# First stage of a two-block transformer kernel: another order of its work, Toeplitz copies in halves, output powers on POOL

## The chip, the cores and the metric

The kernel runs on one core of a Trainium2 chip. The metric is the device time of one execution in microseconds (us). All data are float32. TensorE (PE) multiplies and transposes into PSUM, which has eight banks; VectorE (DVE), ScalarE (ACT) and GpSimd (POOL) work beside it; SyncE (SP), POOL and ACT issue DMAs. Every engine takes its own instructions in program order and meets the others only at semaphores.

## The reference, cut to what matters

The whole program is two transformer blocks with two layers each, on 256 tokens of width 1024. The change is inside the first layer's mixer, a diagonal state space model (S5) with 64 groups of 16 channels and 64 complex states per group:

```
shift1, scale1, gate1, ... = split(silu(c) @ ada_w[0] + ada_b[0], 6)      # "ada": 1024 x 6144
h   = rms_norm(x, norm1_g[0]) * (1 + scale1) + shift1
mix = s5_mixer(h, lam, log_dt, b, c, d, w_glu, b_glu)                     # states over 256 tokens
x   = x + gate1 * mix
...                                                                      # FFN, MLA layer, second block
```

The mixer is computed in chunks of 8 tokens. Inside a chunk the outputs are a product with a Toeplitz matrix built from one row of kernel values; between chunks 31 states follow each other, and each chunk's state is multiplied into its outputs with "output powers", C times powers 1 to 8 of the poles.

## The kernel before

One program per engine, each written out by hand; nothing reorders it. Steps wait for each other by semaphores; PSUM banks are handed out in turn by `next_bank`, and the one who reads a bank out signals `emptied`. The first stage reaches from the start to the first FFN, some 154 us of 1232. Names used below:

- **ada panels**: 1 MB pieces of `ada_w`. Panels 0 to 23 are three blocks of eight. POOL issues their loads (`ada_load`, L2892) into six slots (two in `aring`, four in `ring`), the load of panel i after PE has taken panel i - 6. PE takes a panel with `ada_panels` (eight rows in the trace). `take_row` (ACT) and `row_columns` (PE) turn a block's result into columns; block 0 gives `gmod`, with which x is modulated. Panels 24 and up are used by DVE, late in the FFN.
- **input powers**: DVE, `input_powers(b)` for b = 0 to 3, each two halves of three `tensor_tensor` of 128x1024. PE transposes them (`inputs`), ACT copies them out to `wT`, and they also give the kernel row (`kernel_rows`, `kernel_columns`, the latter at L739 and L742), which ACT writes to the last slice of `toep` (`take_kernel_columns`).
- **Toeplitz copies**: SP, L1561, seven DMAs from that slice to the seven others, each shifted by 16 partitions, after both halves of the kernel row are there. Seven memsets on POOL (L2901) clear what they leave free. `own_inputs` (PE, L828) multiplies with the result.
- **modulated x**: U in `hT`, two DVE operations of 128x2048, then `chunk_inputs(b)` on PE for b = 0 to 3, which ACT copies to `BU` in `sq`.
- **scan**: DVE, 30 steps of a `tensor_tensor` (L1581, sq<-stat,arena) and a `tensor_reduce` (L1826). It starts when all four `chunk_inputs` are out and ends with `states_ready`.
- **output powers**: DVE, `output_powers(b)`, six `tensor_tensor` of 128x1024 each. b = 0 ahead of the scan, b = 1 cut into 24 small pieces inside it, b = 2 and 3 behind it. Each half signals `ca_ready`.
- **end of the stage**: PE, `state_outputs(0)` and `(1)` (L851), `gelu_columns`, `state_outputs(2)`, the first gate products `glu_part` (L872), `state_outputs(3)`, the rest of the gate products, then the FFN.
- x in natural layout is loaded once more (`xN`, L1543, 1 MB) and transposed to `xT` (L799).

Of the kernel before, what the change touches and what calls it, by code (L numbers as in the profile page):

```python
# [10 lines left out]
ALU = mybir.AluOpType  # L11
# [3 lines left out]
P = 128  # L15
# [148 lines left out]
def blocks_kernel(nc, a, constants, out):  # L164

    ctx = ExitStack()
    with ctx:
# [126 lines left out]
        kern = carve(3072, 1024).rearrange("p (x n) -> p x n", n=P)  # L294
# [15 lines left out]
        row0 = toep[:, L5 - 1, 0:512]  # L310
# [4 lines left out]
        wT = [carve(o + (2 + i) * 2048, 2048).rearrange("p (j i n) -> p j i n", i=2, n=P) for i in range(2)]  # L315
# [23 lines left out]
        xN = sq[:, :].rearrange("p (b d) -> p b d", d=D)  # L339
# [280 lines left out]
        def _(eng):  # L620
# [45 lines left out]

            eng.wait_ge(done("b_landed"), 16 * 2)
            coefficient_columns(0)
            vector_columns(0, "s")

# [34 lines left out]
            def inputs(b):  # L705

                eng.wait_ge(done("ab_ready"), 2 * (b + 1))
                for i in range(2):
                    for h in range(2):
                        eng.wait_ge(*next_bank(("w", b, i, h), "s"))  # L710
                        ps = bank_of(("w", b, i, h)).rearrange("p (j n) -> p j n", n=P)
                        for j in range(4):
                            last = eng.transpose(ps[:, j, :], aB[b % 2][:, i, 4 * h + j, :], ident)  # L713
                        last.then_inc(*fills(("w", b, i, h)))
# [18 lines left out]
            def kernel_columns(i):  # L733
# [7 lines left out]
                for x in range(4):  # L741
                    last = eng.matmul(ps[:, x * P:(x + 1) * P], kern[:, 4 * i + x, :], ident, start=False, stop=True,  # L742
                                      skip_group_check=True)
                last.then_inc(*fills(("kernT", i)))

            def chunk_inputs(b):
# [4 lines left out]
                eng.wait_ge(done("u_ready"), 1)  # L751
                eng.wait_ge(*next_bank(("bu", b), "s"))
                ps = bank_of(("bu", b)).rearrange("p (j i c) -> p j i c", j=BJ, i=2)
                for j in range(BJ):
                    for i in range(2):
                        for r in range(2):
                            last = mm(ps[r * N5:(r + 1) * N5, j, i, :], wT[b % 2][:, j, i, r * N5:(r + 1) * N5],
# [5 lines left out]
            ada_panels(0, 2)  # L763
            eng.wait_ge(done("group_rows_ready"), 1)
# [5 lines left out]
            ada_panels(2, 2)  # L770
            eng.wait_ge(done("const5_landed"), 16)
            eng.wait_ge(done("xc_squares"), 8)
            eng.wait_ge(*next_bank("xstat", "s"))
            mm(bank_of("xstat")[:, 0:L5], con5("same_chunk"), ss[:, 0, :]).then_inc(*fills("xstat"))
            ada_panels(4, 1)
            inputs(0)
            kernel_rows(0)
            ada_panels(5, 1)
# [57 lines left out]
            for i in range(4):  # L836
                own_inputs(i // 2, i % 2)
# [2098 lines left out]
```

## Time and profile before

| | us |
|---|---|
| median of 3 runs (1226.98 to 1230.12) | 1229.67 |
| the profiled execution | 1233.93 |
| its span | 1231.7 |
| between span and execution time | 2.2 |

The page gives PE as busy for 95% of the span, DVE 39%, ACT 23%, POOL 4%. In a timeline a line is one instruction or a run of like ones: start, duration, engine, line of the program, operation, out<-in, count, and in brackets the idle time of the engine before it and what ended it. The chain of waits follows the work that ended last back to the start. PEclk is the clock that TensorE was granted, as a share of 2.4 GHz.

### The profile page before, as it was taken

The numbers are of one execution on the slowest core, as the hardware profiler recorded it, in microseconds if no ns is written. First come the engines' busy times: TensorE is split into PE (matmuls) and PEld (weight loads), VectorE is DVE, ScalarE is ACT, GpSimd is POOL, SyncE is SP. The second block draws the span as 40 slices with busy tenths as digits, with TensorE's granted clock in tenths as the row PEclk, the third lists the DMA queues.
The fourth block names the chain that finished last, engine by engine and source line by source line (L and its number), as shares of the span: only waits on it lengthen the run. The fifth ranks groups of instructions, "written<-read, shape, count | busy, mean of one in ns | idle before, by whom it ended". The sixth has DMA issues, their size and how long they took to land.

```text
span 1231.7 us, 19272 instructions
## 1 busy us (share of the span) xinstructions
PE 1164.1 (95%) x8403; PEld 960.1 (78%) x8403; DVE 480.4 (39%) x950; ACT 283.2 (23%) x674; POOL 52.5 (4%) x73
## 2 busy tenths in 40 slices
PE   5876999999999999999999999999999999999997
PEld 3535788888887867688888888788899767886666
DVE  6896264441313428623000000427364542405431
ACT  4521330000002445612000000233122322004431
POOL 2310001110000000000000000000022000000000
PEclk9987999999999899999999999999999999999989
DMA  9969669987643234163535341544410004543210
GB/s 301 367 184 354 216 224 378 357 332 268 250 161 110 103 120 139 36 211 110 192 109 198 104 169 35 164 137 138 134 57 4 3 1 137 196 146 103 66 37 35
DMA packets 120770, 196.68 MB, mean 160 GB/s; under 512 B 5772, under 2 KB 104750, under 8 KB 113262
## 3 DMA queue, kind: packets, MB, share of 16 engines
q1 hardware_dynamic: 110554, 132.20, 33.2%
q0 software_dynamic: 8336, 59.77, 12.7%
q10 hardware_dynamic: 1796, 3.47, 0.9%
q8 instruction: 67, 1.10, 0.4%
q14 instruction: 17, 0.14, 0.0%
HBM read 192.54 MB, written 1.05 MB: 157 GB/s over the span
## 4 chain that ended last, share of the span: by engine, by line
PE 86%; DVE 6%; DMA 3%; ACT 3%; issue 1%; POOL 0%; SPq 0%; DVEq 0%; ACTq 0%
PE psum L624 64%; PE psum L955 12%; PE psum L872 2%; PE psum L1391 2%; ACT arena L2371 2%; DMA ring<-in_ada_w 2%; DMA aring<-in_ada_w 1%; DVE arena L1581 1%; DVE stat L1630 1%; PE psum L1182 1%; DVE arena L1587 1%; PE psum L851 1%; PE psum L713 1%; DVE hT L1581 1%; PE psum L1152 1%
## 5 line engine op out<-in xcount | busy, mean ns | idle before, releaser
L624 PE MATMUL psum<-hT,ring 128*128 128x256 f32 x1392 | 313.2, 382 | 2.9 <-ACT hT L2371 1.8
L624 PEld LDWEIGHTS psum<-hT,ring 128*128 128x128 f32 x1392 | 263.3, 191 | 43.4 <-issue 7.3
L2371 ACT ACTIVATE arena<-psum 128x256 f32<-128x256 f32 (+5 forms) x215 | 96.9, 476 | 654.4 <-PE psum L624 596.0
L624 PE MATMUL psum<-hT,arena 128*128 128x256 f32 (+1 forms) x960 | 162.8, 337 | 2.7 <-DVE hT L1581 2.5
L624 PEld LDWEIGHTS psum<-hT,arena 128*128 128x128 f32 (+1 forms) x960 | 141.4, 176 | 22.9 <-issue 4.2
L1581 DVE TENSOR_TENSOR arena<-arena,psum 128x256 f32<-128x256 f32 (+1 forms) x75 | 39.2, 536 | 296.4 <-ACT arena L2371 267.2
L624 PE MATMUL psum<-arena 64*64 64x64 f32 (+6 forms) x1996 | 111.3, 247 | 2.3 <-issue 1.9
L624 PEld LDWEIGHTS psum<-arena 64*64 64x64 f32 (+4 forms) x1996 | 89.4, 140 | 18.6 <-issue 15.6
L624 PE MATMUL psum<-ring,arena 128*128 128x256 f32 (+2 forms) x320 | 85.8, 433 | 0.5 <-ACT arena L2371 0.5
L955 PE MATMUL psum<-arena,ring 128*128 128x256 f32 x384 | 85.1, 380 | 0.0
L1587 DVE SCALAR_TENSOR_TENSOR acc<-aring,c_act,acc 128x2048 f32<-128x2048 f32 x28 | 65.8, 2349 | 43.8 <-DMA aring<-in_ada_w 25.4
L955 PEld LDWEIGHTS psum<-arena,ring 128*128 128x128 f32 x384 | 72.7, 190 | 12.3 <-issue 2.5
L624 PEld LDWEIGHTS psum<-ring,arena 128*128 128x128 f32 x320 | 64.5, 203 | 21.2 <-issue 8.3
L955 PE MATMUL psum<-arena 128*128 128x256 f32 x320 | 70.7, 379 | 0.0
L955 PEld LDWEIGHTS psum<-arena 128*128 128x128 f32 x320 | 60.6, 190 | 8.1
L1581 DVE TENSOR_TENSOR arena<-arena 128x512 f32<-128x512 f32 (+8 forms) x94 | 60.6, 662 | 2.3 <-PE psum L624 0.4
L2917 POOL TENSOR_TENSOR arena<-arena 128x1536 f32<-128x1536 f32 x4 | 13.8, 3440 | 545.4 <-DVE arena L1581 533.9
L624 PE MATMUL psum<-arena,ring 128*128 128x256 f32 x160 | 35.0, 380 | 0.5 <-DVE arena L2069 0.5
L624 PEld LDWEIGHTS psum<-arena,ring 128*128 128x128 f32 x160 | 30.3, 190 | 4.8 <-DVE arena L2069 0.8
L2371 ACT ACT_TABLE_LOAD x25 | 32.1, 1283 | 7.7 <-DVE arena L1584 4.8
L2371 ACT ACTIVATE arena<-arena 128x256 f32<-128x256 f32 (+8 forms) x48 | 26.6, 576 | 22.6 <-DVE arena L2312 13.8
L872 PE MATMUL psum<-hT,ring 128*128 128x256 f32 x128 | 28.4, 381 | 1.3 <-DVE hT L1841 1.3
(232 smaller groups left out, 1120.7 us busy)
## 6 DMA issues: line engine op xcount, KB each, us to landing
aring<-in_ada_w POOLq DMA_DIRECT2D x32, 1024.0 KB, 7.6
ring<-in_ada_w POOLq DMA_DIRECT2D x16, 1024.0 KB, 14.9
ring<-in_a_w_in SPq DMA_DIRECT2D x14, 1024.0 KB, 5.4
arena<-in_ffn_w_gate SPq DMA_DIRECT2D x12, 1024.0 KB, 8.2
arena<-in_ffn_w_up SPq DMA_DIRECT2D x12, 1024.0 KB, 8.3
ring<-in_ffn_w_down SPq DMA_DIRECT2D x12, 1024.0 KB, 5.0
ring<-in_ffn_w_gate SPq DMA_DIRECT2D x10, 1024.0 KB, 9.5
ring<-in_ffn_w_up SPq DMA_DIRECT2D x10, 1024.0 KB, 6.6
```

The costliest lines, as they stand in the source:

```text
L624: return eng.matmul(dst, w, x, start=first, stop=last)
L713: last = eng.transpose(ps[:, j, :], aB[b % 2][:, i, 4 * h + j, :], ident)
L851: last = eng.matmul(y5_at(kh, r, k4, x), st[n5, :, i, j], c[n5, j, :, :], start=False, stop=i == 1, skip_group_check=True)
L872: last = eng.matmul(ps[:, m, :], w[:, k, m * P:(m + 1) * P], hT3[:, k, :], start=m == 0 and k == 0, stop=k == KC - 1, skip_group_check=True)
L955: last = eng.matmul(dn[c // 2][:, c % 2, :], w[:, kk, c * P:(c + 1) * P], hid[:, 2 * j + kk, :], start=(j == 0 and kk == 0 and c % 2 == 0) ...
L1152: last = eng.transpose(ps[0:DQK, h, :], x[:, b, 4 * g + h, :], ident)
L1182: eng.matmul(ps[r, 0:T], v1[:, 0, h * DV:(h + 1) * DV], head_t[:, h % 2, 0:T], start=True, stop=False, skip_group_check=True)
L1391: last = eng.matmul(ps[:, j, :], out0[i][0][:, k, j * P:(j + 1) * P], mixT[0][:, k, :], start=(i > 1 and j == 0 and k == 0), stop=(k == (K ...
L1581: return V.tensor_tensor(dst, x, y, op)
L1587: return V.scalar_tensor_tensor(dst, x, s, y, op0, op1)
L2371: return eng.activation(dst, x, f, **k)
L2917: G.tensor_tensor(lt_m7[l % 2], lt7, mask.unsqueeze(1).to_broadcast([P, NU, CR]), ALU.mult)\
```

## The change

- SP: the load of `xN` is gone. The Toeplitz copies go in two halves of 512 columns, seven DMAs each; the first half waits for the first half of the kernel row only.
- PE: `xT` is made by transposing `xC_in`, the chunked x that is loaded anyway, ahead of panel 2. `inputs` is split in two, the panels are spread between its pieces, `kernel_columns(0)` comes before `inputs(2)`, `own_inputs` comes half by half with panels 20 to 23 behind each half. Five 128x256 matmuls on constants (`keep_warm`) follow the first vector columns.
- DVE: three of the seven memsets are at the start; four on POOL at the start. `group_rep` is made after `input_powers(0)`. x is modulated in halves of 32 groups (`u_ready` 1 and 2) with half of `input_powers(3)` between. All output powers are gone.
- POOL: all output powers, eight halves of three `tensor_tensor` of 128x1024, between the panel loads.
- ACT: the copies follow PE's new order. `wT` has three places, `kern` two.

```diff
-            def inputs(b):
-                eng.wait_ge(done("ab_ready"), 2 * (b + 1))
+            def inputs(b, i):
+                eng.wait_ge(done("ab_ready"), 2 * b + i + 1)
...
-            for i in range(4):
-                own_inputs(i // 2, i % 2)
-            ada_panels(20, 4)
+                eng.wait_ge(done(f"toeplitz{i}_landed"), 16 * (L5 - 1))
+                for r in range(2):
+                    own_inputs(i, r)
+                ada_panels(20 + 2 * i, 2)
...
-                eng.wait_ge(done("ca_ready"), 2 * (b + 1) + (BJ - 2 if b else 0))
+                eng.wait_ge(done("ca_ready"), 2 * (b + 1))
...
-            sp.dma_start(xN, a["x"][0].rearrange("(b p) d -> p b d", p=P)).then_inc(done("x_landed"), 16)
...
             for i in range(2):
                 sp.wait_ge(*emptied_at(("kernT", i)))
-            for t in range(L5 - 1):
-                n = P5 * (t + 1)
-                sp.dma_start(toep[P - n:P, t, :], toep[0:n, L5 - 1, :]).then_inc(done("toeplitz_landed"), 16)
+                for t in range(L5 - 1):
+                    n = P5 * (t + 1)
+                    sp.dma_start(toep[P - n:P, t, 512 * i:512 * i + 512], toep[0:n, L5 - 1, 512 * i:512 * i + 512])\
+                      .then_inc(done(f"toeplitz{i}_landed"), 16)
...
+            modulate(0)
+            input_powers(3, (1,))
+            modulate(1)
...
-            output_powers(0)
             for b in range(NB5):
                 eng.wait_ge(*emptied_at(("bu", b)))
...
-            output_powers(2)
-            output_powers(3)
...
+            def output_powers(b, i, temp, loads=(0, 0, 0)):
+
+                js, k9 = slice(b * BJ, (b + 1) * BJ), slice(1, L5 + 1)
+                dst = (ca_re, ca_im)[i][:, js]
+                temp = temp.rearrange("p (j k q) -> p j k q", k=L5, q=P5)
+                if g.last:
+                    eng.wait_ge(*g.last)
+                for n, (to, pw, co) in enumerate(((dst, powr, ct[:, i]), (temp, powi, ct[:, 1 - i]))):
+                    G.tensor_tensor(to, pw[:, k9, js].rearrange("p k j -> p j k").unsqueeze(3).to_broadcast([P, BJ, L5, P5]),
+                                    co[:, js, :].unsqueeze(2).to_broadcast([P, BJ, L5, P5]), ALU.mult).then_inc(*g.step())
+                    ada_loads(loads[n])
+                eng.wait_ge(*g.last)
+                G.tensor_tensor(dst, dst, temp, (ALU.add, ALU.subtract)[i]).then_inc(*g.signals("ca_ready"))
+                ada_loads(loads[2])
...
+            output_powers(0, 1, ahead, (0, 1, 1))
+            eng.wait_ge(done("xc_scaled"), 8)
+            for h in range(2):
+                for y in range(2):
+                    eng.wait_ge(*filled_at(("xT", h, y)))
+            output_powers(0, 0, ahead, (0, 1, 1))
+            ada_loads(5)
+            eng.wait_ge(done("u_ready"), 2)
+            output_powers(1, 0, behind, (0, 1, 1))
+            output_powers(1, 1, behind, (1, 0, 1))
+            ada_loads(1)
+            eng.wait_ge(*filled_at(("bu", 2)))
+            output_powers(2, 0, behind)
+            eng.wait_ge(*filled_at(("kernT", 1)))
+            output_powers(2, 1, behind)
+            for i in range(2):
+                output_powers(3, i, behind)
```

**POOL, from panel 18's load to the last output power.** In the program before, POOL has only loads here; these are panels 16 to 24 and on (bank 3 filled means that PE has finished a block):

```order
L2892 DMA aring<-in_ada_w 128x2048 [waits early_used] x2
L2892 DMA ring<-in_ada_w 128x2048 [waits early_used]
L2892 DMA ring<-in_ada_w 128x2048 [waits bank3_filled]
L2892 DMA ring<-in_ada_w 128x2048 [waits early_used] x2
L2892 DMA aring<-in_ada_w 128x2048 [waits early_used] x2
```

In the changed program the same stretch is (L2912 and L2916 are the output powers, L2894 the loads; the first row is panel 18, the next load panel 19):

```order
L2894 DMA aring<-in_ada_w 128x2048 [waits early_used]
L2912 TENSOR_TENSOR arena<-arena,acc 128x1024 [waits ca_ready,u_ready]
L2912 TENSOR_TENSOR arena<-stat,acc 128x1024
L2894 DMA aring<-in_ada_w 128x2048 [waits early_used]
L2916 TENSOR_TENSOR arena<-arena 128x1024 [waits gpsimd_step]
L2894 DMA ring<-in_ada_w 128x2048 [waits early_used]
L2912 TENSOR_TENSOR arena<-arena,acc 128x1024 [waits ca_ready]
L2894 DMA ring<-in_ada_w 128x2048 [waits bank3_filled]
L2912 TENSOR_TENSOR arena<-stat,acc 128x1024
L2916 TENSOR_TENSOR arena<-arena 128x1024 [waits gpsimd_step]
L2894 DMA ring<-in_ada_w 128x2048 [waits early_used] x2
L2912 TENSOR_TENSOR arena<-arena,acc 128x1024 [waits ca_ready,bank0_filled]
```

Eleven more `tensor_tensor` stand behind the last of these rows, then panel 24. So loads and output powers now hold each other up: panel 19's load waits for PE to take panel 13, which PE does behind `chunk_inputs(3)`, and everything below it waits too.

**PE, around the Toeplitz products.** Before, one wait for all copies stands ahead of all products (L828), and panels 20 to 23 behind them:

```order
L624 MATMUL psum<-aring,c_act 32x512 [waits ada_panel0_landed]
L624 MATMUL psum<-aring,c_act 32x512 x3
L624 MATMUL psum<-aring,c_act 32x512 [waits ada_panel1_landed]
L624 MATMUL psum<-aring,c_act 32x512 x3
L828 MATMUL psum<-arena,hT 32x128 [waits bank7_emptied,bank6_emptied,bank4_emptied,toeplitz_landed,toeplitz_clear]
```

In the changed program (products at L844) each half has its wait and two panels behind it:

```order
L844 MATMUL psum<-arena,hT 32x128 [waits toeplitz0_landed,bank4_emptied,bank5_emptied,toeplitz_clear]
L844 MATMUL psum<-arena,hT 32x128 x15
L844 MATMUL psum<-arena,hT 32x128 [waits bank5_emptied]
L844 MATMUL psum<-arena,hT 32x128 x15
L625 MATMUL psum<-ring,c_act 32x512 [waits ada_panel2_landed]
L625 MATMUL psum<-ring,c_act 32x512 x3
L625 MATMUL psum<-ring,c_act 32x512 [waits ada_panel3_landed]
L625 MATMUL psum<-ring,c_act 32x512 x3
L844 MATMUL psum<-arena,hT 32x128 [waits bank6_emptied,toeplitz1_landed,bank7_emptied]
```

The copies of the first half no longer wait for the second half of the kernel row, and the products no longer stand in front of panels 20 and 21.

## Rows read from the trace of the kernel before

**Rows 1.** The page: busy time by engine, and PE in 40 slices.
```profile
span 1231.7 us, 19272 instructions
PE 1164.1 (95%) x8403; PEld 960.1 (78%) x8403; DVE 480.4 (39%) x950; ACT 283.2 (23%) x674; POOL 52.5 (4%) x73
...
PE   5876999999999999999999999999999999999997
```

**Rows 2.** Chain of waits, 70 to 160 us: start, us, what.
```profile
78.19 14.03 DMA aring<-in_ada_w
...
94.19 7.17 issue
101.36 5.99 PE psum L828 x128
```

**Rows 3.** Windows: stretch, length, then each engine's busy us, clock, DMA share, GB/s.
```profile
84.00:101.00 17.00, 3.87 (x16) 0.40 (x16) 16.24 (x47) 0.00 (x0) 1.06 (x2) 0.55 1.02 310
```

**Rows 4.** Timeline of SP, and the copies' times to landing (L1561).
```profile
75.72 5.56 SPq L1561 DMA_DIRECT2D arena<-arena  x7
...
DMA to landing us min/median/max: 2.9/10.8/20.7
```

**Rows 5.** Timeline of PE, 60 to 150 us.
```profile
68.66 2.06 PE L624 MATMUL psum<-hT,arena 128*64 128x32 f32 x64
70.65 1.12 PE L739 MATMUL psum<-acc,const_sb 16*128 16x512 f32 x2
71.70 1.16 PE L742 MATMUL psum<-const_sb,arena 128*128 128x128 f32 x8
...
112.08 3.36 PE L851 MATMUL psum<-arena 64*32 64x128 f32 x128
...
127.31 1.98 PE L851 MATMUL psum<-arena 64*32 64x128 f32 x64
```

**Rows 6.** Timeline of DVE: first wait, ada columns, output powers, scan steps, output powers again.
```profile
5.74 0.26 DVE L1643 COPY stat<-psum 128x96 f32<-128x96 f32 x1 [4.29 <-PE psum L624]
...
46.31 0.29 DVE L1581 TENSOR_TENSOR arena<-psum,arena 128x128 f32<-128x128 f32 x1 [4.10 <-PE psum L693]
...
71.73 0.29 DVE L1581 TENSOR_TENSOR sq<-stat,arena 128x128 f32<-128x128 f32 x1
...
94.39 0.29 DVE L1581 TENSOR_TENSOR sq<-stat,arena 128x128 f32<-128x128 f32 x1
...
95.12 0.29 DVE L1581 TENSOR_TENSOR sq<-stat,arena 128x128 f32<-128x128 f32 x1
...
98.67 1.21 DVE L1581 TENSOR_TENSOR arena<-arena,acc 128x1024 f32<-128x1024 f32 x1
...
111.64 1.22 DVE L1732 TENSOR_TENSOR arena<-arena 128x1024 f32<-128x1024 f32 x1
```

**Rows 7.** Timeline of PE, 20 to 60 us.
```profile
31.62 1.94 PE L624 MATMUL psum<-ring,c_act 128*32 128x512 f32 x8 [1.49 <-DMA ring<-in_ada_w]
...
38.33 1.03 PE L624 MATMUL psum<-ring,c_act 128*32 128x512 f32 x8
41.04 2.00 PE L784 MATMUL psum<-const_sb,arena 128*128 128x128 f32 x16 [1.67 <-ACT arena L2371]
...
45.61 0.66 PE L693 MATMUL psum<-const_sb,arena 128*128 128x128 f32 x4 [0.72 <-ACT arena L2371]
...
55.58 3.92 PE L624 MATMUL psum<-hT,arena 128*64 128x32 f32 x128 [2.47 <-DVE hT L1581]
```

**Rows 8.** Timeline of POOL: memsets, a load, a tensor_tensor.
```profile
8.09 1.25 POOL L2892 DMA_DIRECT2D aring<-in_ada_w  x2 [5.54 <-DMA arena<-in_s_b_im]
...
31.23 6.30 POOL L2901 MEMSET arena<- 112x1024 f32 x7 [0.76 <-DVE arena L1771]
...
76.47 0.53 POOL L2892 DMA_DIRECT2D ring<-in_ada_w  x1 [10.01 <-PE psum L624]
...
913.70 3.43 POOL L2917 TENSOR_TENSOR arena<-arena 128x1536 f32<-128x1536 f32 x1 [533.89 <-DVE arena L1581]
```

More of the change, by code:

```diff
@@ L665, in coefficient_columns, with keep_warm @@
                     last.then_inc(*fills(("raw", m, h)))
+            def keep_warm(n, pool="a"):
+                b = POOLS[pool][turns[pool] % len(POOLS[pool])]
+                eng.wait_ge(emptied[b], bank_uses[b])
+                for _ in range(n):
+                    mm(psum[:, b, 0:T], ones, const_sb[:, 0:T])
             eng.wait_ge(done("b_landed"), 16 * 2)
@@ L763, in _ @@
             ada_panels(0, 2)
+            eng.wait_ge(done("xc_landed"), 16 * 4)
+            for h in range(2):
+                for y in range(2):
+                    key = ("xT", h, y)
+                    eng.wait_ge(*next_bank(key, "b"))
+                    ps = bank_of(key).rearrange("p (s n) -> p s n", n=P)
+                    for x in range(4):
+                        last = eng.transpose(ps[:, x, :], xC_in[:, 4 * y + x, h * P:(h + 1) * P], ident)
+                    last.then_inc(*fills(key))
+            ada_panels(2, 1)
+            inputs(0, 0)
+            eng.wait_ge(done("const5_landed"), 16)
+            eng.wait_ge(done("xc_squares"), 8)
+            eng.wait_ge(*next_bank("xstat", "s"))
+            mm(bank_of("xstat")[:, 0:L5], con5("same_chunk"), ss[:, 0, :]).then_inc(*fills("xstat"))
+            inputs(0, 1)
+            kernel_rows(0)
+            ada_panels(3, 1)
             eng.wait_ge(done("group_rows_ready"), 1)
@@ L785, in _ @@
                 last.then_inc(*fills(("U", i)))
+            ada_panels(5, 1)
+            inputs(1, 1)
+            kernel_rows(1)
             ada_panels(6, 2)
             row_columns(0, row_of[0], "s")
-            inputs(1)
-            kernel_rows(1)
+            kernel_columns(0)
+            inputs(2, 0)
             eng.wait_ge(*emptied_at(("ada", 0)))
@@ L1634, in _ @@
             V.memset(rows[:, :], 0.0).then_inc(*v.signals("rows_clear"))
+            for t in range(3):
+                V.memset(toep[0:P - P5 * (t + 1), t, :], 0.0).then_inc(*v.signals("toeplitz_clear"))
             def vector_columns(i):
@@ L2895, in _ @@
             G.memset(c_half, 0.0).then_inc(*g.signals("halves_clear"))
+            for t in range(3, L5 - 1):
+                G.memset(toep[0:P - P5 * (t + 1), t, :], 0.0).then_inc(*g.signals("toeplitz_clear"))
             eng.wait_ge(done("b_landed"), 16 * 2)
@@ new lines, in _, with ada_loads @@
+            begun = [10]
+            def ada_loads(n):
+                for _ in range(n):
+                    ada_load(begun[0])
+                    begun[0] += 1
+            ahead, behind = sq[:, 1024:2048], tmp5[:, 0:1024]
+            for h in range(2):
+                eng.wait_ge(*emptied_at(("raw", 1, h)))
+            eng.wait_ge(done("xc_squares"), 8)
+            eng.wait_ge(*filled_at("xstat"))
+            eng.wait_ge(*filled_at("grp"))
+            output_powers(0, 1, ahead, (0, 1, 1))
@@ L2904, in _ @@
+            eng.wait_ge(*filled_at(("kernT", 1)))
+            output_powers(2, 1, behind)
+            for i in range(2):
+                output_powers(3, i, behind)
             for i in range(EARLY, len(ada_source)):
```

186 lines of the change are left out of this document (76 added, 110 removed).

## The prediction

> **What bounds the kernel now.** I read the page first: PE is busy for 1164 of 1231.7 us, and the only slices of PE that are not at 9 are the first four and the last [rows 1]. So the time can only come from the first stage, and what it loses or gains there moves everything behind it one for one. The chain of waits says where: from 78.2 us it runs over a panel's load (14.0 us), then 7.2 us of waiting without an engine to name, then the Toeplitz products [rows 2]. That wait is the Toeplitz copies: seven issues from 75.7, the last at 80.6, landing 20.7 us later, 101.3 [rows 4], and the products start at 101.36 [rows 2]. From 84 to 101 us PE works 3.9 of 17 us, its clock is granted 0.55, and the DMA engines are full [rows 3]. DVE runs its scan to 98.7 and output powers to 112.9 [rows 6]. PE's `state_outputs(0)` start at 112.08, `state_outputs(3)` at 127.31 [rows 5]: 15.2 us of nearly full PE work between them. I take `state_outputs(3)` as the mark; behind it nothing changes, so its shift is the change in time.
>
> **Part 1, copies in halves and panels earlier.** The second half of the kernel row is now issued right behind the change's `kernel_columns(1)`, near 69 us, the first half some 20 us before. Copies for 0.9 MB beside fewer panels land, at the 10.8 us median of the copies [rows 4], by 85 at the latest; even with the 20.7 us of the slowest, 94. Panels 20 to 23 (about 1.0 us each when warm [rows 7]) leave the stretch behind the products. So copies and panels no longer set the start of `state_outputs(0)`; next late is the scan.
>
> **Part 2, when the scan starts.** It needs `chunk_inputs(3)`, on PE to 70.7 before [rows 5], scan from 71.73 [rows 6]. PE now does more ahead of it: both `kernel_columns` (2 x (1.12 + 1.16), about 4.4 us [rows 5]) and two more panels (about 1.0 each when warm [rows 7]): +6.4. It loses waits: 1.67 and 2.47 [rows 7], 0.72 at the row columns [rows 7], and up to 1.5 at panel loads [rows 7] since 1 MB of x is no longer loaded: -4.8 to -6.3. That makes 71 to 73; I take 71.5. DVE is not late for this: it had 4.1 us of idle ahead of the ada columns at 46.3 [rows 6], which half of `input_powers` now fills, so the second half of U is ready near 58 and PE wants it at about 64. The early matmuls show a second thing: a panel takes 1.93 us until 32 us and 1.03 at 38 [rows 7], half speed although the clock row reads 1.00. `keep_warm` may end that sooner. It lies in a gap that PE has anyway ahead of the C coefficients, so it costs nothing; what it may bring (0.9 us for each of five panels) goes mostly into waits for loads. I take 0, and keep -2.
>
> **Part 3, the scan.** A step is 0.73 us where nothing is between (94.39 to 95.12); from 71.73 to 94.39 the 24 steps with a piece of output powers in them take 0.94 each, so 24 of 30 steps lose 0.21: -5 us [rows 6], and `output_powers(0)` (six of 1.2 us [rows 6]), which filled the time in which DVE waited for `chunk_inputs(3)` anyway, is gone. So 30 x 0.73 = 22 us, `states_ready` at 93.5 instead of 98.7. If nothing else held it, `state_outputs(0)` would come at about 94.5 instead of 112.1: -17.6 us. This is the floor.
>
> **Part 4, output powers on POOL.** The only price is L2917: 3.43 us for 1536 columns [rows 8], so 2.29 for 1024, if it scales. Bounds: 0.9, a memset of 1024 (6.30 / 7 [rows 8]), which reads nothing, and 3.43 itself. I take 2.3, the same operation. Load and powers are in one queue: panel 19's load waits for panel 13, which PE takes behind `chunk_inputs(3)`, about 71.5. Behind it stand 16 `tensor_tensor` and 5 loads: 16 x 2.3 + 5 x 0.53 [rows 8] + 16 hand-overs of about 0.1 = 41 us, so the last half is ready at 112.5. PE wants it at `state_outputs(3)`, 94.5 + 15.2 = 109.7. `state_outputs(1)` wants its part at 96 and gets it at 82, `(2)` wants 98.5 and gets it at 98.5. So PE waits 2.8 us and the mark is at 112.5 instead of 127.3: -14.8. PE has pauses before 94 and at 110; before, the clock was down after a pause of like length, so I add 1 of lost clock: **-14**. With 0.9 for each the floor holds, -17.6; with 3.43 the last half is ready at 130.5: +3. Panels 24 and 25 come 20 us later than before, but DVE wants them only in the FFN. The four memsets (0.9 each) and three on DVE lie in the first 8 us, where POOL waits 5.5 us for the B coefficients and DVE 4.3 for the poles [rows 6, 8]: 0; if uncovered they would delay panel 0 by under 1 us.
>
> POOL's first `tensor_tensor` now stands in the middle of the panel loads, and no row shows what a first one costs, since the one at 913.7 had 534 us of idle ahead of it [rows 8]. The Trainium skill (GPSIMD Engine Reference, section Instruction dispatch) says that the first call of a newly loaded routine pays for loading its code, about 6 us. By that page panels 10 to 13 would come up to 6 us later, and the sum would be -14 plus at most 3, since PE has three us of slack at panel 10.
>
> **Rivals.** *A: POOL and DVE keep each other out.* Nothing in the trace excludes it: all four POOL `tensor_tensor` run while DVE is idle or has an operand in PSUM, so no row shows two readers of SBUF side by side. The memsets from 31.23 [rows 8] ran beside DVE powers at the usual length, but they read nothing. Say a DVE `tensor_tensor` with both inputs in SBUF waits until POOL's ends. Then each of the 16 POOL operations behind panel 13 lets one scan step through: 16 x (2.3 + 0.2) = 40 us, the other 14 steps 10 us, scan 50 us, `states_ready` at 122, mark at 137: +10. The first six POOL operations (13.8 us) also fall on the input powers, of which 6 are slack: +8 more at most. I take **+13**, 1243, slower. It decides from about ten held steps: 10 x 1.8 = 18 us use up the 17.6 of the floor. For it speaks that the scan's `tensor_tensor` reads `stat` and `arena`, both in SBUF; against it, no row. The Trainium skill (SBUF — State Buffer, section Who interferes with whom) states just this: a VectorE instruction with two SBUF inputs contends with a GpSimd instruction that reads SBUF, and the second one is blocked for the whole instruction. By that page the result is case A; no row here shows it.
>
> *B: POOL's layouts are slow.* The powers are read with a stride and broadcast, which L2917 was not. At 2.8 to 3.4 us each the mark is between -6 and +3: 1223 to 1233.
>
> *C: nothing waits for POOL.* At 2.1 us or less the floor holds: 1212.
>
> *D: the front gets later.* If panels 9 to 12 are short of POOL loads, because loads queue behind powers, the scan starts at 76 and not 71.5 and everything shifts by 4.5: -9.5, 1220. It is in the range of the forecast.
>
> **How the numbers follow.** The profiled execution, 1233.93, would become 1219.9; against the median of 1229.67 that is 1215.7, and I give all numbers against the median. Chances: forecast with C and D, 0.50, its own range 1210 to 1221; B 0.13, half of it a gain and half within 0.3% (3.7 us, about what a measurement of this kernel can tell from no change); A 0.37, 1235 to 1249, of which 0.01 falls within 0.3%. So faster 0.565, same 0.075, slower 0.36. The range must take in A to hold 8 in 10: 1209 to 1247. Most of the chance lies at its two ends, not in its middle.
>
> **What would show it.** Right: the scan's step at 0.73 us from first to last, starting at 70 to 74; POOL's 128x1024 at 2.3; `state_outputs(0)` at 94 to 96; the chain of waits runs over POOL just before `state_outputs(3)`. A: scan steps of about 2.5 us while POOL is busy and 0.73 afterwards, and DVE `tensor_tensor` of 128x1024 longer than 1.22 between 40 and 58 us. B: POOL's operations over 2.8. D: PE waits on `ada_w` loads between 50 and 70. It would be wrong altogether if PE still waited for copies at the products, or if the front, where I count PE by sums, lost more than 5 us.

## The result, and the profile after

| | before | after |
|---|---|---|
| median of 4 runs each, same chip (us) | 1229.7 (1226.98 to 1230.12) | 1248.98 (1247.49 to 1249.32) |
| ratio, 95% interval | 1 | 1.0159 [1.0142, 1.0177] |
| span of the profiled execution | 1231.7 | 1245.7 |
| first scan step starts | 71.7 | 81.6 |
| scan, 30 steps | 27.0 | 49.7 |
| `state_outputs(3)` starts (the mark) | 127.3 | 147.4 |

The change makes the kernel 19.3 us slower. I had forecast 1216, faster; the result is also 2 us above the top of my range. The mark moved by 147.4 - 127.3 = +20.1, so all of it lies in the first stage, as I had assumed. One execution of e1_order_only below (1717.1 us) ran in a slow state of the chip, at a granted clock of 0.65, and is in none of the figures here.

The timeline of PE after the change (start, us, engine, line, operation; in brackets the idle time ahead and what ended it):

```profile
55.20 0.79 PE L625 MATMUL psum<-arena 128*128 128x128 f32 x2 [6.44 <-DVE arena L1590]
59.02 1.94 PE L625 MATMUL psum<-ring,c_act 128*32 128x512 f32 x8 [3.03 <-DVE arena L1590]
...
98.79 1.93 PE L844 MATMUL psum<-arena,hT 128*32 128x128 f32 x64
...
131.35 4.79 PE L867 MATMUL psum<-arena 64*32 64x128 f32 x128 [24.12 <-DVE arena L1821]
...
147.36 1.98 PE L867 MATMUL psum<-arena 64*32 64x128 f32 x64
```

The wait for the Toeplitz copies is gone: the products (L844, the second half shown) are done by 100.7 without a wait of their own. PE's waits that matter are for DVE, three times: 6.4 and 3.0 us in the input powers and 24.1 us for the scan's last reduce (L1821). (It also waits 3.7 us for a panel's load at 91.55, which costs nothing, since the scan ends much later.) The answer to [rows 5] is that `state_outputs(0)` now stands at 131.35 instead of 112.08.

The timeline of DVE, first the input powers (L1590 and L1743), then the scan (L1590 `tensor_tensor`, L1821 `tensor_reduce`):

```profile
42.45 3.29 DVE L1743 TENSOR_TENSOR arena<-arena 128x1024 f32<-128x1024 f32 x1
45.67 3.04 DVE L1590 TENSOR_TENSOR arena<-arena 128x1024 f32<-128x1024 f32 x1
48.63 3.04 DVE L1590 TENSOR_TENSOR arena<-stat,arena 128x1024 f32<-128x1024 f32 x1
51.70 3.24 DVE L1743 TENSOR_TENSOR arena<-arena 128x1024 f32<-128x1024 f32 x1
...
55.07 1.21 DVE L1590 TENSOR_TENSOR arena<-arena 128x1024 f32<-128x1024 f32 x1
...
81.62 0.29 DVE L1590 TENSOR_TENSOR sq<-stat,arena 128x128 f32<-128x128 f32 x1
81.94 0.38 DVE L1821 TENSOR_REDUCE arena<-sq 128x64 f32<-128x192 f32 x1
82.35 2.71 DVE L1590 TENSOR_TENSOR sq<-stat,arena 128x128 f32<-128x128 f32 x1
...
85.51 4.72 DVE L1590 TENSOR_TENSOR sq<-stat,arena 128x128 f32<-128x128 f32 x1
...
117.91 1.98 DVE L1590 TENSOR_TENSOR sq<-stat,arena 128x128 f32<-128x128 f32 x1
...
120.33 0.29 DVE L1590 TENSOR_TENSOR sq<-stat,arena 128x128 f32<-128x128 f32 x1
...
130.92 0.37 DVE L1821 TENSOR_REDUCE arena<-sq 128x64 f32<-128x192 f32 x1
```

And POOL, its first block beside the input powers and three of the operations beside the scan (L2912 products, L2916 sums, L2894 panel loads):

```profile
34.01 2.09 POOL L2912 TENSOR_TENSOR arena<-arena,acc 128x1024 f32<-128x1024 f32 x1 [0.44 <-PE psum L625]
36.06 3.01 POOL L2912 TENSOR_TENSOR sq<-stat,acc 128x1024 f32<-128x1024 f32 x1
39.02 0.59 POOL L2894 DMA_DIRECT2D ring<-in_ada_w  x1
39.63 5.03 POOL L2916 TENSOR_TENSOR arena<-arena,sq 128x1024 f32<-128x1024 f32 x1
...
85.44 2.05 POOL L2912 TENSOR_TENSOR arena<-arena,acc 128x1024 f32<-128x1024 f32 x1
87.42 0.59 POOL L2894 DMA_DIRECT2D ring<-in_ada_w  x1
88.03 2.04 POOL L2912 TENSOR_TENSOR arena<-stat,acc 128x1024 f32<-128x1024 f32 x1
```

Read the two together. A `tensor_tensor` of 128x1024 on DVE takes 1.21 us where POOL has none (55.07), and four in a row beside POOL's take 3.0 to 3.3. A scan step's `tensor_tensor` of 0.29 us ends just after a POOL operation does: the one at 85.51 ends at 90.23, behind POOL's two of 85.44 and 88.03 (the second ends at 90.07), with a load between them. The `tensor_reduce` keeps its 0.37 to 0.38. Once POOL's last is out (119.7), the scan is back at 0.29 and 0.73 a step. That is rival A's picture. It goes both ways in the front: POOL's sum of 39.63 takes 5.03 us instead of the 2.35 that it takes beside the scan, and in that time two DVE `tensor_tensor` of 128x1024 pass at their usual 1.2 us.

Sums over stretches of the trace say the same, for the input powers, of the held scan and of its free end (stretch, length, busy us of PE, PEld, DVE, ACT, POOL, granted clock, DMA share, GB/s):

```profile
36.00:55.00 19.00, 10.39 (x102) 6.52 (x102) 18.90 (x10) 9.41 (x15) 18.32 (x10) 0.93 0.74 262
82.00:120.00 38.00, 18.21 (x216) 8.07 (x208) 37.04 (x29) 3.10 (x7) 37.23 (x22) 0.70 0.82 269
120.30:131.30 11.00, 0.00 (x0) 0.00 (x0) 9.98 (x32) 0.00 (x0) 0.50 (x1) 0.50 0.51 191
```

DVE is "busy" for 37.0 of 38 us with 29 instructions, and POOL for 37.2. A profile counts a held instruction as busy; only its length against its length elsewhere tells that it was held. The last row also has PE idle at a granted clock of 0.50, the 1.2 GHz level, and while `state_outputs(0)` runs the mean granted clock is 0.68, where it was 1.00 before: it takes 4.79 us where it took 3.36 [rows 5].

### The profile page after: what moved, and what is told of

It is laid out like the page before. It is cut to its first block, busy times and chain, and to the rows that moved or that the text cites. A ratio compares the mean times of both kernels' runs of the same rounds, so it can differ in the third digit from the quotient of the medians.

```text
span 1245.7 us, 19292 instructions
## 1 busy us (share of the span) xinstructions
PE 1158.7 (93%) x8413; PEld 956.8 (77%) x8413; DVE 495.4 (40%) x913; ACT 285.0 (23%) x674; POOL 106.4 (9%) x94
## 4 chain that ended last, share of the span: by engine, by line
PE 83%; DVE 12%; ACT 3%; DMA 1%; issue 1%; SPq 0%; DVEq 0%; POOL 0%; ACTq 0%
PE psum L625 62%; PE psum L964 12%; DVE sq L1590 3%; PE psum L888 2%; DVE arena L1590 2%; PE psum L1400 2%; ACT arena L2361 1%; DMA aring<-in_ada_w 1%; DVE arena L1743 1%; DVE arena L1821 1%; DVE stat L1639 1%; PE psum L1191 1%; PE psum L867 1%; DVE arena L1596 1%; PE psum L1161 1%
## 5 line engine op out<-in xcount | busy, mean ns | idle before, releaser
L625 PE MATMUL psum<-hT,ring 128*128 128x256 f32 x1392 | 311.9, 381 | 3.4 <-ACT hT L2361 2.3
L1590 DVE TENSOR_TENSOR arena<-arena,psum 128x256 f32<-128x256 f32 (+1 forms) x75 | 39.2, 536 | 295.4 <-ACT arena L2361 267.5
L625 PE MATMUL psum<-ring,arena 128*128 128x256 f32 (+2 forms) x320 | 83.0, 422 | 0.5 <-ACT arena L2361 0.5
L1590 DVE TENSOR_TENSOR arena<-arena 128x512 f32<-128x512 f32 (+8 forms) x86 | 59.1, 707 | 1.9
L2894 POOL DMA_DIRECT2D aring<-in_ada_w x32 | 17.3, 542 | 231.2 <-DVE acc L1596 112.7
L1590 DVE TENSOR_TENSOR sq<-stat,arena 128x128 f32<-128x128 f32 x30 | 36.5, 1215 | 1.0
```

Source lines behind the costliest of these rows:

```text
L625: return eng.matmul(dst, w, x, start=first, stop=last)
L1590: return V.tensor_tensor(dst, x, y, op)
L2894: eng.dma_start(early_slots[slot], ada_source[i]).then_inc(ada_landed[slot], 16)
```

## The experiments

Rows of the table: the median in us, its difference to the kernel before on the same chip, and from the trace where the scan starts, how long it takes and where the mark stands.

| kernel | us | to before | ratio, 95% | scan starts | scan | mark |
|---|---|---|---|---|---|---|
| e1_order_only | 1213.2 | -16.4 | 0.9873 [0.9848, 0.9898] | | | |
| e5_order_profile, the same kernel, one run | 1215.3 | -14.6 | | 70.8 | 27.0 | 114.4 |
| e2_pool_only | 1241.1 | +11.5 | 1.0094 [1.0077, 1.0112] | 72.4 | 50.0 | 139.0 |
| e3_scan_psum | 1220.8 | -8.8 | 0.9942 [0.9921, 0.9962] | 84.0 | 22.0 | 122.6 |
| e4_memset | 1213.9 | -15.7 | 0.9870 [0.9856, 0.9885] | 73.3 | 22.0 | 110.7 |
| e6_block_later | 1247.2 | +17.3 | 1.0143 [1.0113, 1.0173] | 71.6 | 58.4 | 146.1 |
| e12_unheld_all_pool | 1225.0 | -3.8 | 0.9965 [0.9951, 0.9980] | 71.1 | 22.0 | 121.9 |
| e7_one_block | 1211.3 | -18.6 | 0.9852 [0.9819, 0.9885] | 74.0 | 22.0 | 113.9 |
| e10_loads_behind | 1211.5 | -18.4 | 0.9852 [0.9828, 0.9876] | 71.0 | 22.0 | 111.1 |
| e9_no_warm | 1216.0 | -13.9 | 0.9889 [0.9870, 0.9907] | 72.8 | 27.0 | 116.8 |
| e11_whole_copies | 1218.2 | -11.7 | 0.9913 [0.9888, 0.9939] | 69.8 | 27.0 | 115.3 |

The scan's start differs by some 4 us (69.8 to 74.0) between kernels whose front holds nothing, so marks of single traces are good to a few us; the medians are the firmer column. The ratio is one of means, so it can differ by 1 or 2 us from the difference of the medians.

**The two halves of the change apart.** e1_order_only is the changed kernel with the output powers on DVE again, at the places of before, and POOL with loads and memsets only.

```diff
+            output_powers(0)
             for b in range(NB5):
                 eng.wait_ge(*emptied_at(("bu", b)))
...
+                if u < 6 * BJ // 2:
...
+            output_powers(2)
+            output_powers(3)
```

> The changed kernel with the output powers back on DVE, at the places they had before (b = 0 ahead of the scan, b = 1 in pieces inside it, b = 2 and 3 behind it); POOL has loads and memsets only. Theory (POOL's and DVE's readers of SBUF keep each other out): with no tensor_tensor on POOL nothing is held. Input powers end near 58 us, the scan starts at 71 to 73, steps of 0.94 and 0.73, states_ready at 98 to 100, state_outputs(3) at 116 to 118 instead of 127.3 before: 1219. Rival 1 (the new order of the front is what costs, POOL is innocent): the scan starts at about 81 as in the changed kernel, and the time is 1238 to 1245.

> The same kernel as e1_order_only (the change's order of the first stage, output powers on DVE as before, POOL with loads and memsets only), run once more for its trace. Expected, by either theory: 1215 us; first scan step at 73 (as in e4_memset, whose first reduce is at 73.6), the scan at 0.94 us a step while it has pieces of output powers between, so its end near 100.5; state_outputs(0) right behind it; state_outputs(3) at 112 to 114 (127.3 before), since all of the 14.4 us that e1_order_only gained should show at that mark. No DVE tensor_tensor of 128x1024 above 1.25 us.

e2_pool_only is the kernel before with all output powers on POOL: b = 0 after the input powers, b = 1 to 3 after the second half of the kernel row.

> The kernel before, in its old order, with all output powers on POOL: b = 0 from the end of the input powers on, the rest behind the load of panel 23. Theory: two steps of the scan held at its start, free while POOL issues loads, then some 17 steps of about 2.15 us; states_ready near 120 instead of 98.7, state_outputs(3) 8 to 10 us later: 1238 to 1240. Rival 1: the scan keeps 0.73 us a step, states_ready near 95, but the Toeplitz copies hold the products as before: 1229 to 1231.

The new order alone gains 16.4 us by the median of e1_order_only, 15.6 by its ratio, 14.6 in e5_order_profile; I take 15.6. (The 14.4 in the expectation above comes from a median with the execution of 1717.1 us in it.) Output powers on POOL alone cost 11.5. Together they cost 19.3, not -4.1. So moving the powers costs some 35 us in the new order and 11.5 in the old one. The timeline of DVE, then PE, in e2_pool_only tells why:

```profile
84.83 4.32 DVE L1581 TENSOR_TENSOR sq<-stat,arena 128x128 f32<-128x128 f32 x1
...
121.97 0.37 DVE L1810 TENSOR_REDUCE arena<-sq 128x64 f32<-128x192 f32 x1
```
```profile
100.86 6.32 PE L828 MATMUL psum<-arena,hT 128*32 128x128 f32 x128 [5.09 <-issue]
...
122.40 5.39 PE L851 MATMUL psum<-arena 64*32 64x128 f32 x128 [10.42 <-DVE arena L1810]
```

In the old order the scan had room, since `state_outputs(0)` came at 112.1 anyway, 13.3 us after it [rows 5, 6]; a scan that ends at 122.3 costs only what lies beyond that. Five of POOL's 24 also run between the input powers and the scan there (61.3 to 72.3); DVE is idle until 71.7, so next to nothing is held. The new order takes that room away, and the changed kernel puts POOL's first six beside the input powers.

In e5_order_profile, the same kernel as e1_order_only, PE (first row) waits for the scan, and the mark (last row) is 12.9 us ahead of before:

```profile
97.87 5.29 PE L867 MATMUL psum<-arena 64*32 64x128 f32 x128 [4.85 <-DVE arena L1850]
...
114.41 1.98 PE L867 MATMUL psum<-arena 64*32 64x128 f32 x64
```

**Is it the read of SBUF by both?** e4_memset replaces each POOL `tensor_tensor` by two memsets of the same output: it leaves the output powers out and puts a constant in their places. That keeps POOL busy nearly as long (two memsets take 2.0 us) and reads nothing.

```diff
-                    G.tensor_tensor(to, pw[:, k9, js].rearrange("p k j -> p j k").unsqueeze(3).to_broadcast([P, BJ, L5, P5]),
-                                    co[:, js, :].unsqueeze(2).to_broadcast([P, BJ, L5, P5]), ALU.mult).then_inc(*g.step())
+                    for _ in range(2):
+                        if g.last:
+                            eng.wait_ge(*g.last)
+                        G.memset(to, 0.01).then_inc(*g.step())
```

> The changed kernel, with each tensor_tensor of POOL's output powers replaced by two memsets of the same 128x1024 output (the output powers are left out, their places hold a constant). POOL is busy nearly as long, writes the same places, waits and signals at the same points, and reads nothing. Theory (reads are what collide): input powers of 1.22 us throughout, scan start 71 to 73, steps of 0.73, states_ready at 93 to 95, state_outputs(3) at 110 to 112: 1213 to 1215. Rival 2 (any POOL work, or its waits in the load queue, slows DVE): held steps, 1235 or more.

It came out at 1213.9. Its DVE timeline has no held operation, from the scan's first step to its last 22.0 us:

```profile
73.31 0.29 DVE L1590 TENSOR_TENSOR sq<-stat,arena 128x128 f32<-128x128 f32 x1
73.63 0.37 DVE L1821 TENSOR_REDUCE arena<-sq 128x64 f32<-128x192 f32 x1
```

e3_scan_psum leaves POOL as in the change and takes the other reader away: the scan's multiplier `step4` lies in PSUM bank 2, so the `tensor_tensor` of the scan has one SBUF input. The input powers keep two. To free that bank, the vector and row columns on PE take turns in two banks instead of three, and DVE makes `step4` just ahead of the scan.

```diff
-        step4 = small[:, 0:4, :].rearrange("p (e i) j -> p e i j", e=2)
+        step4 = psum[:, 2, 0:4 * J5].rearrange("p (e i j) -> p e i j", e=2, i=2)
```

> The changed kernel, with the four pole rows that every scan step reads (step4) in a PSUM bank instead of SBUF, so that the scan's tensor_tensor has one input in SBUF; POOL's work is unchanged, and so is DVE's work ahead of the scan. Theory (only two SBUF inputs are held): scan start 82 as in the changed kernel, all 30 steps 0.73 to 0.8 us, states_ready near 105, POOL's last output power near 119, state_outputs(3) at 121 to 123: 1225. Rival 2 (POOL's arithmetic slows DVE in another way: bandwidth, semaphores, anything that does not depend on the operand's place): steps stay at 2 us and more, 1245 to 1250.

1220.8: beside the same POOL operations the scan takes 22.0 us instead of 49.7, 0.29 us for each `tensor_tensor`, while the input powers are held as in the changed kernel and the scan still starts some 12 us late, at 84.0. The new location of one operand is worth 28 us.

e8_pairs measures the disputed cost by itself: it leaves out the whole transformer and has only DVE and POOL operations on 128 rows.

> Not the transformer: only pairs of operations on 128 rows. DVE alone: tensor_tensor of 1024 columns with both inputs in SBUF, the same of 128 columns, of 1024 with one input in PSUM, copy of 1024. POOL alone: tensor_tensor of 1024, copy of 1024. Then side by side, started together, no waits in between: eight DVE tensor_tensor (SBUF, SBUF) beside four POOL tensor_tensor; 24 of 128 columns beside four; eight with one PSUM input beside four; eight copies beside four; eight tensor_scalar beside four; 24 reduces (3 x 64) beside four; eight DVE tensor_tensor beside four POOL copies; beside four POOL memsets. Theory (exclusion needs a DVE instruction with two SBUF inputs and a POOL instruction that reads SBUF): only the DVE tensor_tensor with both inputs in SBUF are held, and only beside POOL's tensor_tensor and copy, some 1.5 to 4 us each until POOL is done; every other pair runs at its times alone, within 5%. Rival (any DVE instruction that reads SBUF twice or once contends, or POOL's writes too): copies, reduces or the pair with memset are longer as well.

Its timeline, alone first, then pairs (n instructions in one row; POOL's and DVE's start together):

```profile
12.89 6.90 DVE L23 TENSOR_TENSOR vc<-va,vb 128x1024 f32<-128x1024 f32 x6
...
28.68 3.70 DVE L25 COPY vc<-va 128x1024 f32<-128x1024 f32 x6
...
32.59 9.23 POOL L28 TENSOR_TENSOR gc<-ga,gb 128x1024 f32<-128x1024 f32 x4 [3.86 <-DVE vc L59]
...
42.12 3.98 POOL L29 COPY gc<-ga 128x1024 f32<-128x1024 f32 x4
...
46.30 17.75 DVE L23 TENSOR_TENSOR vc<-va,vb 128x1024 f32<-128x1024 f32 x8 [4.19 <-POOL gc L76]
46.42 13.15 POOL L28 TENSOR_TENSOR gc<-ga,gb 128x1024 f32<-128x1024 f32 x4
...
78.06 9.14 DVE L24 TENSOR_TENSOR vc<-psum,vb 128x1024 f32<-128x1024 f32 x8
...
87.50 13.48 DVE L25 COPY vc<-va 128x1024 f32<-128x1024 f32 x8 [0.17 <-POOL gc L76]
...
114.97 6.80 DVE L27 TENSOR_REDUCE vc<-va 128x64 f32<-128x192 f32 x24
...
124.39 12.53 DVE L23 TENSOR_TENSOR vc<-va,vb 128x1024 f32<-128x1024 f32 x8 [2.49 <-POOL gc L76]
124.49 7.95 POOL L29 COPY gc<-ga 128x1024 f32<-128x1024 f32 x4
...
137.16 9.17 DVE L23 TENSOR_TENSOR vc<-va,vb 128x1024 f32<-128x1024 f32 x8
```

Eight DVE `tensor_tensor` from SBUF take 8 x 1.15 = 9.2 us alone, 17.75 beside four of POOL, and POOL's four take 13.15 instead of 9.23: they take turns, about 3.3 us a pair. With one input in PSUM (9.14) or beside POOL's memsets (9.17) nothing is held; beside POOL's copies it is (12.53, and POOL's 7.95 instead of 3.98). The pair with 128 columns has the form that matters for the scan; DVE's groups of instructions in the time of POOL's four, 64.3 to 73.6 (busy us, mean ns of one, idle):

```profile
L23 DVE TENSOR_TENSOR vc<-va,vb 128x128 f32<-128x128 f32 x4 | 9.5, 2431 | 0.1
```

Four DVE operations, 0.22 us each alone, in the 9.3 us of POOL's four, at 2.4 us each: exactly one for each of POOL's. My expectation missed in two pairs: DVE's copies, 0.62 us each alone, are held as well (13.48 us for eight), and eight `tensor_scalar` are as long (13.50; they have no row alone). The condition is not two SBUF inputs alone. The Trainium skill (SBUF — State Buffer, section Who interferes with whom) names both cases, two SBUF inputs and the copies and `tensor_scalar` that use both port pairs; these rows agree with it, down to PSUM operands and memsets being free.

**Where does the front's part come from?** e6_block_later moves POOL's first block behind U, so that all 24 stand behind it.

```diff
-            output_powers(0, 1, ahead, (0, 1, 1))
...
-            output_powers(0, 0, ahead, (0, 1, 1))
-            ada_loads(5)
+            ada_loads(9)
...
             eng.wait_ge(done("u_ready"), 2)
+            output_powers(0, 1, behind, (0, 1, 1))
+            output_powers(0, 0, behind, (1, 0, 1))
```

> The changed kernel with POOL's first six output powers (b = 0) moved from beside the input powers to behind both halves of U, so that all of POOL's 24 stand beside the scan. Theory (each SBUF-reading POOL tensor_tensor holds one DVE tensor_tensor with two SBUF inputs, wherever they meet): the input powers take 1.22 each again and the scan starts at 73 instead of 81.6, but 20 to 22 steps of it are held instead of 14, at about 2.4 us each: 21 x 2.4 + 9 x 0.73 = 57 us, end at 130 to 133; state_outputs(3) at 146 to 149, 1247 to 1251 us, within 0.3% of the changed kernel. Rival (it was the place that cost: the front has PE behind it, the scan has room): the front's 8 to 10 us come back, 1239 to 1241.

The scan starts at 71.6 instead of 81.6: the front was worth 10.0 us. But 20 of its steps are held instead of 14 and it takes 58.4 us instead of 49.7; the end is nearly the same, 1247.2 against 1249.0. Wherever a POOL operation meets a held DVE operation on the path it costs about the same: six in the front 10.0 us, 1.7 each; 16 beside the scan 49.7 - 22.0 = 27.7 us, 1.7 each; in e6_block_later 22 of them 36.4, 1.7 each.

e12_unheld_all_pool is e6_block_later with `step4` in PSUM as well.

> e6_block_later (all 24 of POOL's output powers behind U) with the scan's multiplier (step4) in PSUM as in e3_scan_psum, so that POOL holds neither the input powers nor the scan. It is the case that my prediction took as likeliest, POOL's own pace setting state_outputs(3), with 22 powers behind panel 19's load instead of 16. Theory, by the prediction's Part 4 with the measured durations: scan from 73 to 95; POOL 22 x 2.2 us and five loads from 72, end of the last power at 121.5 to 123, PE waits for it just before state_outputs(3) at 122 to 123.5 (127.3 before), so -4 to -5 us: 1224 to 1226 us. Rival (PE is not waiting for POOL but for something else of this order, so the end follows the scan as in e4_memset): state_outputs(3) at 111 to 114, 1214 to 1217 us. Against e6_block_later it also shows what the held steps cost once POOL's work is the same: 21 to 25 us by the theory.

1225.0: against before, each on its chip, 21 us less than e6_block_later with the same work on POOL. This is the case that I had forecast as likeliest, with 22 operations behind panel 19's load instead of 16, and here PE does wait for POOL's pace:

```profile
93.20 1.98 PE L867 MATMUL psum<-arena 64*32 64x128 f32 x64 [0.50 <-DVE arena L1824]
...
108.87 3.59 PE L867 MATMUL psum<-arena 64*32 64x128 f32 x64 [8.88 <-POOL arena L2917]
112.40 7.17 PE L888 MATMUL psum<-hT,ring 128*128 128x256 f32 x32
121.90 3.15 PE L867 MATMUL psum<-arena 64*32 64x128 f32 x64 [2.33 <-POOL arena L2917]
```

**Terms of the sum.** e9_no_warm is e5_order_profile without `keep_warm(5, "s")`.

> The order of e1_order_only and e5_order_profile (output powers on DVE) without the five constant matmuls of keep_warm. My prediction took 0 for them, with up to 2 us of gain. In the program before, five panels between 19 and 33 us take 1.93 us each where warm ones take 1.06; with keep_warm the third is at 1.24. By the prediction's term: 1215 to 1217 us, the panels up to 32 us at 1.93, the scan's start within 2 us of e5_order_profile's 70.8. Rival (the early clock is what the new order lives on, since PE is what the scan's start waits for): scan's start 3 us or more later, 1218 us or more.

1216.0; by the ratios that is 2 us above e1_order_only, with intervals that overlap, so the five matmuls bring nothing that these runs resolve. Without them the third panel takes 1.07 us and the fourth 1.52; with them, in e5_order_profile, the third takes 1.24, the fourth 1.04, and the first two 1.93 all the same. In the trace of the changed kernel, which has the same five matmuls, the first two take 1.06 and 1.39, so single traces don't settle what they do. My rival (a scan 3 us later) doesn't hold either: it starts at 72.8, inside the scatter.

e11_whole_copies gives e5_order_profile its Toeplitz copies back in one piece.

```diff
-                for t in range(L5 - 1):
-                    n = P5 * (t + 1)
-                    sp.dma_start(toep[P - n:P, t, 512 * i:512 * i + 512], toep[0:n, L5 - 1, 512 * i:512 * i + 512])\
-                      .then_inc(done(f"toeplitz{i}_landed"), 16)
+            for t in range(L5 - 1):
+                n = P5 * (t + 1)
+                sp.dma_start(toep[P - n:P, t, :], toep[0:n, L5 - 1, :]).then_inc(done("toeplitz_landed"), 16)
```

> The order of e5_order_profile with the Toeplitz copies whole again (seven DMAs of 1024 columns after both halves of the kernel row, both halves of the products waiting for them; panels 20 and 21 still between the halves). In e5_order_profile the last kernel column is out near 68, the fourteen issues run from 47.9 to 72.3, the products are at 78.8 and 86.8, and PE waits 4.9 us for the scan at 97.9. By the prediction's term (the copies no longer set state_outputs(0), with 10.8 us median and 20.7 us longest landing): issued 67 to 73, landed by 85 to 94, the products a few us later, state_outputs(0) still at the scan's end: 1215 to 1217 us, so the halves bring 0 to 2 and the order brings the rest. Rival (the halves are what takes the copies off the path): products at 94 or later, state_outputs(0) at 101 or later, 1219 us or more.

Between the two: 1218.2, against before 3 us (e5_order_profile) to 5 us (e1_order_only) above the kernel with halves (the intervals of the two ratios overlap between 0.9888 and 0.9898, so this is not firm). PE's timeline suggests the reason:

```profile
89.63 3.64 PE L844 MATMUL psum<-arena,hT 128*32 128x128 f32 x64 [9.76 <-DMA arena<-arena]
...
99.99 3.37 PE L868 MATMUL psum<-arena 64*32 64x128 f32 x128
```

The copies land at 89.6, inside my 85 to 94, but the work behind them then ends at 100.0, 3.2 us after the scan (96.8). So of the order's 15.6 us some 3 to 5 belong to the halves, and some 11 or 12 to the rest of the order.

**A version that beats both.** e7_one_block has the powers b = 0, 2 and 3 on DVE, b = 1 on POOL after DVE's b = 0, and `step4` in PSUM. e10_loads_behind puts POOL's panel loads behind five of its six powers.

> The order of e1_order_only (output powers 0, 2 and 3 on DVE), with b = 1 on POOL from the moment that DVE has finished b = 0, and the scan's multiplier (step4) in PSUM, so that no tensor_tensor of the scan has two SBUF inputs. Theory: the 24 pieces leave the scan (24 x 0.21 = 5 us), nothing in it is held, and POOL's six take 2.05 to 2.35 each and end before state_outputs(1): scan at 0.73 us a step, end at 95 to 96, state_outputs(3) 5 us earlier than in e5_order_profile, 1210 us. Rival (POOL slows DVE in the scan through its writes and its reduce, which read and write SBUF, whatever the tensor_tensor reads): steps of 1 us or more beside POOL, 1213 us or more.

> e7_one_block with POOL's queue in another order: its six output powers (b = 1) first, and the loads of panels 19 to 23 behind the fifth of them instead of in between. In e7_one_block the scan ends at 95.9 but PE is at state_outputs(0) only at 98.4, because panels 22 and 23 (91.7 and 94.7) waited 3.6 and 1.9 us for their loads, which stood behind powers that waited for panel 19's load. Theory (that queue is the last 2.5 us): panels 20 to 23 come without those waits, state_outputs(0) right at the scan's end, and 1 to 2.5 us less than e7_one_block: 1209 to 1210 us. Rival (the DMA engines are busy then anyway): panels as late as before, 1211 us.

1211.3 and 1211.5: 18.6 and 18.4 us faster than before, some 38 than the change. The 24 pieces leave the scan (27.0 to 22.0 us) and nothing is held. Over e1_order_only, with nothing but loads and memsets on POOL, the gain is not resolved: 0.9852 [0.9819, 0.9885] against 0.9873 [0.9848, 0.9898]. In e7_one_block panels 22 and 23 wait 3.6 and 1.9 us for loads, and `state_outputs(0)` starts 2.4 us behind the scan's end (96.0):

```profile
91.74 1.06 PE L625 MATMUL psum<-ring,c_act 128*32 128x512 f32 x8 [3.56 <-DMA ring<-in_ada_w]
94.66 1.94 PE L625 MATMUL psum<-ring,c_act 128*32 128x512 f32 x8 [1.85 <-DMA ring<-in_ada_w]
...
98.36 4.32 PE L867 MATMUL psum<-arena 64*32 64x128 f32 x128
```

e10_loads_behind did not mend that in the time: its waits at those panels are 0.56 and 1.52 us, another panel waits 4.12, and the median is the same. My expectation of 1 to 2.5 us less was wrong; what limits those loads stays open.

## Why the prediction was wrong

**The step that failed** is Part 3's "if nothing else held it": 30 steps of 0.73 us, 22 us, `states_ready` at 93.5. The scan took 49.7 us and ended at 131.3, and PE waited 24.1 us for it; POOL, whose pace Part 4 had as the limit, was done at 119.7. Behind that stands a choice between two cases: POOL and DVE do keep each other out, and I had put the case without that at 0.50 against 0.37. My reason was that no row of before shows two readers of SBUF side by side. That was true, and it is no evidence against exclusion: a trace in which the two never met can't speak for either. What I should have weighed is what each case costs. With the exclusion every POOL operation beside the scan costs 1.7 us, 27.7 in all, against 17.6 to be gained at most. I had worked out this condition myself ("about ten held steps"); 14 were held, and six more in the front. The section of the Trainium skill that I cited for rival A (SBUF — State Buffer, Who interferes with whom) states the rule for just this pair of readers, and by it the result is case A.

**Rival A's size.** It gave 1243 and the time was 1249. Its scan was right: 50 us forecast, 49.7 measured, though not by 16 single holds but by 14 holds, some of them through two POOL operations. From the scan's end to the mark it had 15 us, measured 16.1, of which 1.4 is the clock lost in the 24 us of waiting. What was mis-sized is the front: "+8 more at most", of which I took 3 in "+13". It measured 10.0 (81.6 against 71.6 in e6_block_later). I had called 6 us of it slack without naming a row; the nearest is the 4.1 us that DVE idled before [rows 6]. But the new order had already spent that idle: Part 2 of my own text fills it with half of `input_powers`. The changed order with nothing held (e4_memset) shows a single DVE pause, of 1.3 us, between 31.9 and 57.2. The six DVE operations that are held in the front take 18.2 us instead of 7.3, and PE's two waits, 6.4 and 3.0, pass that on. With 10 instead of 3 the rival gives +20, and the mark moved by 20.1; that it fits to 0.1 is luck, since single marks are good to a few us. The top of the range, 1247, came from the same term.

**Point by point, the rest.**

- What bounds the kernel, and the mark: right. The profiled spans lie 1 to 6 us lower against before than the marks say, in all kernels the same way (after: span +14.0, mark +20.1), in part because the profiled execution of before was itself 4.2 us above its median; the shifts of the marks are within 1 us of those of the medians for the change and within 5.2 for all.
- Part 1, copies off the path: right; in the changed kernel the products end 30 us before `state_outputs(0)`. That the halves may matter by 3 to 5 us in the new order I had not seen.
- Part 2, scan's start at 71.5 without exclusion: 69.8 to 74.0 in the eight traces of the new order in which nothing is held ahead of the scan. The sum has a slip: 4.56 and 2.0 are 6.6, not 6.4, and its terms give 71.8 to 73.5, so 71.5 was a little below them.
- Part 3, 22 us for the scan without pieces: 22.0 in e3_scan_psum, e4_memset, e10_loads_behind and e12_unheld_all_pool. The floor of -17.6 was -15.7 in e4_memset. The forecast's own case, 16 powers behind panel 19 with nothing held, was not run; -3.8 with 22 of them (e12_unheld_all_pool) and this floor lie to both sides of the -14.
- Part 4, 2.3 us for an operation on POOL: products 2.02 to 2.07, sums 2.34 to 2.38 where nothing holds them. POOL's pace setting `state_outputs(3)` is real, in e12_unheld_all_pool, where the last operation ends at 121.8 (expected 121.5 to 123).
- Rival B is refuted: the strided and broadcast products are the faster ones (2.03 against 2.35). Rival D: the front was late, but by held DVE operations, not by loads.
- The first POOL `tensor_tensor` had 0.44 us of idle ahead of it and took 2.09 us. The 6 us that the Trainium skill (GPSIMD Engine Reference, section Instruction dispatch) gives for the first call of a newly loaded routine don't appear in this kernel.
- `keep_warm`: 0 fits; a gain of some 2 us is not excluded.

## What to carry over

Before work goes to POOL, list what DVE does in the same stretch by its operands: beside a POOL `tensor_tensor` or copy, which read SBUF, a DVE `tensor_tensor` with two SBUF inputs waits for the whole of it (a DVE copy or `tensor_scalar` was held beside POOL's `tensor_tensor` too), so that a chain of short DVE operations goes on at POOL's pace, one step for each. Where the chain can't move, one input in PSUM frees it. And when two edits are costed together, look for the slack that both use: the order that makes one of them pay may be what takes away the other's cover.

## What the runs showed of the hardware that I had not expected

- A DVE operation of 0.29 us can wait through two POOL operations: 4.72 us at 85.51, where a panel load stands between them, and 4.66 at 93.08, where POOL issued loads just ahead of them (the same in e2_pool_only, 4.32 at 84.83, and at both places in e6_block_later, 4.71 and 4.66). Away from loads each POOL operation lets one DVE operation through, 1.6 to 2.0 us each. That a load takes DVE's turn away is a guess from these five places; no run tests it, and loads alone hold nothing (0.29 us steps beside them in e2_pool_only, 76.8 to 82.6).
- The waiting goes both ways when DVE's operations follow each other closely: POOL's two sums took 5.03 and 2.71 us beside the input powers and 2.35 beside the scan.
- Copies and `tensor_scalar` on DVE are held beside POOL's `tensor_tensor` too (a copy 0.62 us alone, 1.69 on average there). Whether its reads or its writes do it is not shown: e8_pairs has no copy beside POOL's memsets.
- POOL's `tensor_tensor` of 128x1024 takes 2.03 us as a product with broadcast operands and 2.35 as a sum of plain ones. It is not the sum: a product of plain operands takes 2.31 in e8_pairs. Why plain operands are slower stays open.
